# A two-layer hybrid backbone on one core: four modulation slices moved behind the latent down pass's tiles, and the first two wide chunks computed side by side

## The reference, cut to what matters

```python
mod = silu(c) @ w_mod[l] + b_mod[l]             # six vectors of 1024: sh1, sc1, g1, sh2, sc2, g2
h = modulate(rms_norm(x, norm1[l]), sh1, sc1)
x = x + g1 * token_mixer(h, ...)                # four branches, gates, w_out
h = modulate(rms_norm(x, norm2[l]), sh2, sc2)   # the second norm
u = h @ w_up[l]                                 # 1024 -> 2 * 2816
a = depthwise_conv(u[..., :D_FF], ...)          # width 3 over the tokens
x = x + g2 * ((silu(a) * u[..., D_FF:]) @ w_down[l])
```

## Time and profile before

| what | value |
|---|---|
| median of three runs | 2977.11 us |
| time of the profiled execution | 2974.92 us |
| its span in the profile | 2973.1 us |
| mean granted TensorE clock | 0.949 of full speed |
| TensorE busy | 2723.3 us, 92% of the span |
| VectorE busy | 1331.9 us, 45% |
| GpSimd busy | 1521.3 us, 51% |
| ScalarE busy | 672.7 us, 23% |

### The profile page before, as it was taken

How to read it: one execution, slowest core, us unless ns; L and a number is a source line. 1 busy time by engine, 2 the same in 40 slices (tenths; PEclk the granted TensorE clock), 3 DMA queues, 4 the chain that set the end, 5 groups by cost and what they waited for, 6 DMA issues and landing times.

```text
span 2973.1 us, 38001 instructions
## 1 busy us (share of the span) xinstructions
PE 2723.3 (92%) x15620; PEld 2218.1 (75%) x15620; DVE 1331.9 (45%) x1752; ACT 672.7 (23%) x1134; POOL 1521.3 (51%) x1412
## 2 busy tenths in 40 slices
PE   5899989999898997999989997998989887899999
PEld 2788877867766876888877876886767666688877
DVE  4522166643566826555561235216643667422121
ACT  4311232121245512000120012023222245211110
POOL 2434457522412633566568425556824325488886
PEclk9999999999988998999989998999989888999999
DMA  7422411311311812444333361221212106233322
GB/s 245 149 64 86 114 38 50 87 45 55 101 32 57 255 57 63 122 119 123 114 102 107 98 207 47 82 64 47 75 47 58 50 26 221 76 93 99 96 87 80
DMA packets 361592, 277.84 MB, mean 93 GB/s; under 512 B 10139, under 2 KB 322111, under 8 KB 360908
## 3 DMA queue, kind: packets, MB, share of 16 engines
q1 hardware_dynamic: 359040, 272.57, 30.7%
q10 hardware_dynamic: 1612, 2.75, 0.2%
q0 software_dynamic: 768, 0.09, 0.0%
HBM read 246.01 MB, written 29.36 MB: 93 GB/s over the span
## 4 chain that ended last, share of the span: by engine, by line
PE 79%; DVE 10%; POOL 4%; ACT 3%; DMA 2%; issue 1%; ACTq 0%; SPq 0%; DVEq 0%; POOLq 0%
PE ps L448 18%; PE ps L449 17%; PE ps L450 17%; PE ps L673 4%; PE ps L994 3%; PE ps L604 2%; PE ps L489 2%; PE ps L490 2%; PE ps L491 2%; POOL w_hi L1131 2%; PE ps L693 1%; POOL w_lo L1134 1%; PE ps L953 1%; PE ps L800 1%; PE ps L635 1%
## 5 line engine op out<-in xcount | busy, mean ns | idle before, releaser
L1131 POOL TENSOR_TENSOR w_hi<-ring,tiny 128x512 fp32r<-128x512 f32 x516 | 591.0, 1145 | 1182.8 <-PE ps L450 662.2
L448 PE MATMUL ps<-hh,w_hi 128*128 128x512 f32 (+1 forms) x2272 | 851.9, 375 | 47.1 <-DVE hl L1676 24.1
L1134 POOL TENSOR_TENSOR w_lo<-ring,w_hi 128x512 fp32r<-128x512 f32 (+1 forms) x572 | 789.0, 1381 | 104.4 <-ACT w_hi L1304 63.9
L449 PE MATMUL ps<-hl,w_hi 128*128 128x512 f32 (+1 forms) x2272 | 825.3, 363 | 0.0
L450 PE MATMUL ps<-hh,w_lo 128*128 128x512 f32 (+1 forms) x2272 | 822.6, 362 | 0.0
L448 PEld LDWEIGHTS ps<-hh,w_hi 128*128 128x128 f32 x2272 | 445.4, 196 | 161.2 <-issue 55.4
L450 PEld LDWEIGHTS ps<-hh,w_lo 128*128 128x128 f32 x2272 | 444.7, 196 | 65.1
L449 PEld LDWEIGHTS ps<-hl,w_hi 128*128 128x128 f32 x2272 | 446.3, 196 | 60.2 <-issue 2.0
L489 PE MATMUL ps<-w_hi,hh 128*128 128x256 f32 (+1 forms) x544 | 158.7, 292 | 19.8 <-ACT arena L1284 11.8
L1284 ACT ACTIVATE arena<-ps 128x512 f32<-128x512 f32 (+3 forms) x130 | 76.0, 585 | 417.8 <-PE ps L450 406.3
L448 PE MATMUL ps<-ffh,w_hi 128*128 128x512 f32 x352 | 142.5, 405 | 18.1 <-POOL w_lo L1134 11.6
(11 more groups left out here) (240 smaller groups left out, 3845.9 us busy)
## 6 DMA issues: line engine op xcount, KB each, us to landing
ring<-in_w_in SPq DMA_DIRECT2D x118, 512.0 KB, 4.0
ring<-in_w_mod SPq DMA_DIRECT2D x96, 512.0 KB, 4.0
ring<-in_w_up SPq DMA_DIRECT2D x88, 512.0 KB, 4.1
ring<-in_w_down SPq DMA_DIRECT2D x48, 512.0 KB, 4.0
logits<-arena SPq DMA_DIRECT2D x32, 384.0 KB, 2.3
arena<-logits SPq DMA_DIRECT2D x32, 384.0 KB, 3.8
ring<-in_w_down SPq DMA_DIRECT2D x24, 384.0 KB, 3.4
ring<-in_w_branch SPq DMA_DIRECT2D x16, 512.0 KB, 4.4
```

The costliest lines, as they stand in the source:

```text
L448: pe.matmul(acc, wh[:, k], hi[:, n, x:y], start=n == 0, stop=False)
L449: pe.matmul(acc, wh[:, k], lo[:, n, x:y], start=False, stop=False)
L1131: pool.tensor_tensor(wh[:, 0:count], w, one[:].unsqueeze(2).to_broadcast([P, count, P]), ALU.mult).then_inc(*up("w_lead", ("lead", key, j)))
L1134: pool.tensor_tensor(wl[:, 0:count], w, wh[:, 0:count].bitcast(F32), ALU.subtract).then_inc(*up("w_split", ("split", key, j)))
```

## The change

Two edits, and a generalisation of the norm functions by layer and kind that emits the same instructions as before.

First, the four last slices move in the load order: slice 44+i goes behind chunk 0 of down tile 3+i. VectorE takes each after the residual and squares of tile 2+i. The sum over partitions moves from ahead of down tile 4 to behind context tile 3.

Second, wide chunks 0 and 1 of each layer are computed together: for each k, three products per column range of chunk 0 and then of chunk 1, as soon as `hl` of that k is there. GpSimd splits the two in the order half 0 of both, half 1 of both.

```diff
@@ weight_chunks
         for n in range(3 * KT):
-            order += [("down", l, n // 3, n % 3)] + slices[2 * FT + n:2 * FT + n + 1]
+            order += [("down", l, n // 3, n % 3)] + (slices[2 * FT + n // 3 - 3:2 * FT + n // 3 - 2] if n % 3 == 0 and n >= 9 else [])
@@ tensor engine
+            def two_projections(keys, width, banks_of, each):
+                ends = segs(width)
+                for key, banks in zip(keys, banks_of):
+                    next_chunk(key)
+                    for s, n in room(key, *banks):
+                        pe.wait_ge(s, n)
+                for j in range(2):
+                    for key in keys:
+                        pe.wait_ge(*at(("split", key, j)))
+                    for k in range(KT // 2 * j, KT // 2 * (j + 1)):
+                        for key in keys:
+                            for x, y in ends:
+                                mm = product(psum(key)[:, x:y], key, j, hh, hl, x, y, count=1, first=k, offset=k - KT // 2 * j,
+                                             each=each if key == keys[0] and x == 0 else None)
+                            if k % (KT // 2) == KT // 2 - 1:
+                                mm.then_inc(*up("pe_half", ("half", key, j), *([("full", key)] if j else [])))
...
                 norm(l, 2)
-                for c in range(2 * FT):
-                    projection(("up", l, c), hh, hl, W[l], (2 * (c % 4), 2 * (c % 4) + 1),
-                               each=(lambda k: ("hl", l, 2, k)) if c == 0 else None)
+                two_projections([("up", l, 0), ("up", l, 1)], W[l], [(0, 1), (2, 3)], lambda k: ("hl", l, 2, k))
+                for c in range(2, 2 * FT):
+                    projection(("up", l, c), hh, hl, W[l], (2 * (c % 4), 2 * (c % 4) + 1))
...
                 for u in range(KT):
-                    if l + 1 < DEPTH and u == 4:
-                        sum_of_modulation(l + 1, 5, 6, 7)
                     acc_key = ("down", l, u)
...
+                        if u == 3:
+                            sum_of_modulation(l + 1, 5, 6, 7)
@@ GpSimd, split_until
-                    pair = next(p for p in token_pairs(first[2]) if first[3] in p) if first[0] == "t" else (0,)
+                    if first[0] == "t":
+                        pair = next(p for p in token_pairs(first[2]) if first[3] in p)
+                    else:
+                        pair = (0, 1) if first[0] == "up" and first[2] == 0 else (0,)
@@ vector engine
-                for kind, n, g, k in next_modulation(l)[2 * FT:]:
-                    modulation_step(n, g, k)
                 if l + 1 < DEPTH:
                     for u in range(KT):
-                        residual_of("lat", u)
-                    norm_of("lat")
+                        residual_of(1, 1, "first", u)
+                        for key in next_modulation(l)[2 * FT + u - 2:2 * FT + u - 1] if u >= 2 else []:
+                            modulation_step(*key[1:])
+                    norm_of(1, 1, "first")
```

More of the change, by code:

```diff
@@ L94, in constants @@
     return dict(k_small=small, k_rope=rope, k_dist=dist, k_mask=mask.reshape(P, -1))
+PARTS = {(1, 1): {"first": (0, LAT), "second": (LAT, T)},
+         (0, 2): {"first": (0, LAT), "second": (LAT, T)},
+         (1, 2): {"first": (0, LAT - CTX), "second": (LAT - CTX, LAT)}}
 class Marks:
@@ L305, in bass_hybrid_backbone, with squares_of @@
                2: arena[:, 0:2 * T].rearrange("p (b t) -> p b t", b=2)}
[L307 to L308 removed]
+        def squares_of(l, which, part, k):
+            x, y = PARTS[l, which][part]
+            if part == "first":
+                return sqb[which][:, k % 2, x:y]
+            lo = (8 + k) * T if which == 1 else 5 * T + CTX * k
+            return arena[:, lo:lo + CTX]
         x_scaled = arena[:, 16 * T:24 * T].rearrange("p (t d) -> p t d", t=NT)
@@ L439, in next_chunk, with product @@
                 used[0] += 1
-            def product(acc, key, j, hi, lo, x, y, count=KT // 2, first=0, whole=KT, each=None):
+            def product(acc, key, j, hi, lo, x, y, count=KT // 2, first=0, whole=KT, each=None, offset=0):
                 wh, wl = w_halves(key, j)
@@ L564, in norm, with sum_of_squares @@
                     mm.then_inc(*up("pe_squares", ("squ", l, which, k), *([("full", key)] if k == KT - 1 else [])))
-            def sum_of_squares(part, k):
-                key, (x, y) = ("norm", 1, part), span_of[part]
+            def sum_of_squares(l, which, part, k):
+                key, (x, y) = ("norm", l, which, part), PARTS[l, which][part]
                 if k == 0:
-                    for s, n in room(key, 4 if part == "lat" else 5):
+                    for s, n in room(key, 4 if part == "first" else 5):
                         pe.wait_ge(s, n)
-                pe.wait_ge(*at(("sq", 1, part, k)))
-                pe.matmul(psum(key)[:, 0:y - x], K["ones"], squares_of[part](k), start=k == 0, stop=k == KT - 1).then_inc(
-                    *up("pe_squares", ("squ", 1, part, k), *([("full", key)] if k == KT - 1 else [])))
+                pe.wait_ge(*at(("sq", l, which, part, k)))
+                pe.matmul(psum(key)[:, 0:y - x], K["ones"], squares_of(l, which, part, k), start=k == 0, stop=k == KT - 1).then_inc(
+                    *up("pe_squares", ("squ", l, which, part, k), *([("full", key)] if k == KT - 1 else [])))
             def mean_squares(l, b, n):
@@ L1216, in decays, with norm_of @@
                 act.activation(pp1, pp1, ACT.Ln, bias=1.0).then_inc(*up("act_set", ("softplus",)))
-            def norm_of(part):
-                key, (x, y) = ("norm", 1, part), span_of[part]
+            def norm_of(l, which, part):
+                key, (x, y) = ("norm", l, which, part), PARTS[l, which][part]
                 act.wait_ge(*at(("full", key)))
```

91 lines of the change are left out of this document (52 added, 39 removed).

## The result

| | before | after |
|---|---|---|
| median of nine runs each | 2977.63 us | 2960.51 us |
| profiled execution | 2974.92 us | 2960.51 us |
| its span | 2973.1 us | 2958.7 us |
| mean granted clock | 0.949 | 0.953 |

The ratio of the two is 0.9946, with a 95% interval of 0.9930 to 0.9963: the change makes the kernel 0.54% faster, 17 us by the medians and 14.4 us between the two profiled executions. The forecast was 2962.3 us.

What follows compares the result with a forecast made beforehand. TensorE, busy 92% of the span, was taken as the bound, so time is won only where it waits or runs at the low clock. 5.0 + 0 + 3.4 + 6.4 = 14.8 us gave 2962.3 us, range 2953 to 2973.

Steps and rivals of the forecast that it cites:

- layer 0's pair, at its end: Layer 0's second norm: wide chunks 0 and 1 together complete @1144.9 instead of @1154.2, 9.3 us won.
- wait ahead of chunk 3: Layer 0's wide pass: chunk 3's load stands behind slice 2, so TensorE waits 3.3 us for it.
- low clock behind that wait: Layer 0, after TensorE's wait for chunk 3: the clock falls, 5.3 us at half speed cost 2.6 us.
- layer 0's pair, net: Layer 0's wide chunks 0 and 1 together, after chunk 3's wait and low clock: 3.4 us gain, ends 0.5 and 6.0.
- slices, down pass: Start of layer 0's down pass: moving four slices' loads and steps away gains 5.0 us, ends 1 and 7.
- the moved sum: Sum moved behind context tile 3: takes TensorE 3.46 us in either place, gain 0, bounds 0 to -2 us.
- layer 1's pair: Layer 1's second norm: wide chunks 0 and 1 together gain 6.4 us, ends 3.0 and 6.6.
- cases a and b: Layer 0's down pass: a, `w_hi` still locked out, gain 4.2 us; b, chunk 1's first half split in time, 6.6 us.
- rival A: Down pass: VectorE and GpSimd take turns, 8.6 us; with layer 0's clock staying up, 21.0 us, 2956.1 us; chance 0.17.
- B: Down pass: slices not worth anything, the row locks GpSimd out longer, part gives 1 us; 2966.3 us; chance 0.15.
- D: Down pass: slices used late make the loads behind them late for TensorE; 15 us slower, 2992 us; chance 0.07.
- C: Layer 0's pair a wash through chunk 3's load (0.5), GpSimd's lead in layer 1 lost (3.0); 2968.6 us; chance 0.15.

Runs made afterwards that it cites:

- slices late: The kernel after with the wide pass's modulation slices two places later in the load order: 2957.4 us; with the last sum ahead of down tile 7 too: 2950.21 us.
- pairs-only kernel: The kernel before with wide chunks 0 and 1 computed together, the last four slices and their sum where they were: 2970.53 us.

## Why the prediction was right, and where it was not

| step | predicted | measured |
|---|---|---|
| layer 0's pair, at its end | 9.3 | 9.1 |
| wait ahead of chunk 3 | 3.3 | 3.39 |
| low clock behind that wait | 2.6 | 1.8 |
| layer 0's pair, net | 3.4 | 3.9 |
| slices, down pass | 5.0 | 6.2 |
| the moved sum | 0 (0 to -2) | -1.7 |
| layer 1's pair | 6.4 | 6.1 |
| sum | 14.8 | 14.5 |

The total came closer than its terms: errors of +0.5, +1.2, -1.7 and -0.3 us cancel to 0.3. That closeness is luck, and so is the 2962.3 against 2960.51 us, since the median of the kernel before itself moved 0.5 us between three and nine runs and single ones lie up to 15 us off.

**The pairs.** The steps came as written: no gap in TensorE's products, the last `hl` not waited for, the load of chunk 3 bound by slice 0's use behind chunk 0's convolution. The experiment that moves the slices confirms the cause, since without slice 2 ahead of chunk 3 the wait and the low clock are both gone. The term that was mis-sized is the clock: I had 5.3 us at half speed for 2.6; it was 3.4 us, and they cost 1.8.

**The down pass.** The step that failed is "one wait of 5 to 8 us for `w_lo` within tile 0" (cases a and b). There is none. I had written that the landing was too close to the start of the row to call, and it was: GpSimd asked 0.44 us into it, and the engines took turns, the mechanism of rival A. I had also written that the stall is made by VectorE's 22 instructions and not by the slices; with slice 44 alone put back it returns, so it takes both. Rival A's price was wrong in turn, 8.6 us predicted and 6.2 measured: the row was stretched to 24.8 us, by 11.5 us, and not by eight GpSimd instructions of 1.2 us: most of these took 1.5 to 1.6 us, and some thirteen of them fell into it. The term of 5.0 was near the truth because it lay between 4.2 and 6.6, not because its story held. Case a, a lockout without the slices in the way, was put at 4.2 us; the kernel with slice 44 back, which is nearest to it, shows 3.4. Tile 1's 2.05 us and the cover for the steps behind tiles 2 to 5 held.

**The moved sum.** The cost lay in the bound, but its reason was not the new place. The kernel before had been spared the low clock in its profiled execution; eight of nine others had 3.4 us wherever the sum stood, and one 6.8. A stretch that was at the full clock in one execution was taken as a property of the kernel, though the five other sums in the same trace all had the low clock behind them.

**The rivals.** B fell (the slices alone gave 6.2 us in the down pass), and D (no down tile got longer, residuals 15.9 us apart). C fell in both halves. Of A the mechanism came, its clock and its price did not.

**The rule.** The Trainium skill, page "SBUF — State Buffer", section "SBUF: two separate sides", has the lock held for one instruction. In the turns of the kernel after the trace agrees: GpSimd got in after at most one subtraction. In the kernel with one slice back the trace disagrees, with 12.72 us over 20 subtractions. So the section's words fit the rows with turns and not those with a lockout.

## What to carry to other kernels

A gain at one wait is worth what the next wait leaves of it: chunk 3's load took 5.2 of the 9.1 us, and the same load order, changed in one line, gave them back. Ahead of a row of back-to-back VectorE instructions have GpSimd's next inputs landed and split: row to residual was 21.1 us so, 25.2 to 25.9 when they landed at its start, and 28.7 or more when they landed 1.5 us or later into it. Before a low or full clock at one place is put into a sum, read it at the other places that run the same code, and in a second execution.

## What the runs showed that was not expected

The start of the row does not decide alone. In layer 0 a first request of GpSimd 0.4 us or less into the row gave turns in four kernels, and one 1.5 us or more into it a lockout, unless a wait stood between the subtractions. But in the kernels with the slices late, and in layer 1 of every kernel, GpSimd was inside an instruction when the row began and one subtraction took 1.7 to 1.8 us beside it. Then GpSimd had nothing to do for 4.03 to 6.30 us, and its next request was locked out (for 7.8 to 9.5 us in those without a wait between the subtractions). After a shorter pause the turns went on: in the kernel after, GpSimd was idle for 2.34 us while VectorE made subtractions of 0.68 us one behind the other, and still got in at once.

```profile
1542.18 1.09 POOL L1161 TENSOR_TENSOR w_hi<-ring,tiny 128x256 fp32r<-128x256 f32 x1 [2.34 <-PE ps L462]
```

In the pairs-only kernel a request after three such subtractions, the first of its row, waited 12.31 us, so the number of undisturbed subtractions does not divide the cases. GpSimd's idle time ahead of the request does, in all 18 rows without waits: every request after at most 3.20 us of idle time got in (3.06 to 3.20 at the start of the rows with turns), and every one after 4.03 us or more was locked out (4.59 to 4.69 in the three rows of layer 0 where it came 1.5 to 1.9 us in). In the kernel with waits, requests after 4.68 and 4.96 us got in. That is a pattern read from the traces; no run changes this idle time by itself, and it is not shown as the cause, which stays open.

Layer 1's mixer, the same instructions in all kernels, took from 823.92 to 831.78 us in the ten profiled executions. That is as much as one part of this change is worth, and it is why the parts were read from segments. As each kernel was profiled once, the traces don't tell whether the spread belongs to executions or to kernels; whole executions of the kernel before lie from 2961.72 to 2988.4 us.
